# First attention of a two-block model: value products with the turned weights as stationary operand, and second-part copies on VectorE

## What is computed

```
for i in range(seq // 128):                       # 128 queries against (i + 1) * 128 keys
    z = q_i @ k[:kend].T / sqrt(64)
    mask = kpos < qpos
    log_beta = log_sigmoid(z)
    log_1m_beta = where(mask, log_beta - z, 0)
    suffix = cumsum(log_1m_beta, reverse=True) - log_1m_beta
    a = where(mask, exp(log_beta + suffix), 0)
    o_i = a @ v[:kend]
o = o * silu(z_gate);  x = x + gate * (o @ w_out)
```

## Time and profile before

| | us |
|---|---|
| median of 3 runs | 2759.29 (2758.49 to 2763.61) |
| the profiled execution, whole | 2765.38 |
| its span | 2763.6 |
| first attention in it | about 929.8 to 1210.5 |

### The profile page before, as it was taken

How to read it: one execution, slowest core, us unless ns; L and a number is a source line. 1 busy time by engine, 2 the same in 40 slices (tenths; PEclk the granted TensorE clock), 3 DMA queues, 4 the chain that set the end, 5 groups by cost and what they waited for, 6 DMA issues and landing times.

```text
span 2763.6 us, 34691 instructions
## 1 busy us (share of the span) xinstructions
PE 2596.2 (94%) x12363; PEld 2160.0 (78%) x12363; DVE 1548.8 (56%) x2099; ACT 1110.7 (40%) x1866; POOL 855.5 (31%) x626
## 2 busy tenths in 40 slices
PE   3899999999999999999899998789997999999998
PEld 2688888788778799987788877678875888887887
DVE  5666665641325466657764437775568777771112
ACT  3400001431411488856643437661265555551000
POOL 1233332012233466630132220233102323225664
PEclk7999999999999999999999999999999999999999
DMA  5244444344166544434253337414242333339933
GB/s 217 82 147 138 137 137 122 98 155 135 69 230 193 139 111 110 111 116 151 84 183 130 107 125 178 157 44 168 77 145 76 107 107 107 122 98 301 295 91 123
DMA packets 377272, 374.81 MB, mean 136 GB/s; under 512 B 36323, under 2 KB 284556, under 8 KB 376972
## 3 DMA queue, kind: packets, MB, share of 16 engines
q1 hardware_dynamic: 346844, 303.91, 37.0%
q10 hardware_dynamic: 30256, 68.69, 6.6%
HBM read 286.55 MB, written 85.98 MB: 135 GB/s over the span
## 4 chain that ended last, share of the span: by engine, by line
PE 75%; DVE 13%; ACT 5%; DMA 4%; issue 1%; POOL 1%; SPq 0%; ACTq 0%; DVEq 0%; POOLq 0%
PE PS L1743 27%; PE PS L1828 22%; PE PS L1897 8%; PE PS L801 5%; PE PS L779 2%; DMA mod_raw<-in_w_ada 2%; PE PS L1810 2%; PE PS L1787 1%; PE PS L765 1%; PE PS L764 1%; DVE opBf L2938 1%; DVE M L2599 1%; PE PS L1942 1%; DVE prob L1176 1%; ACT opBf L2085 1%
## 5 line engine op out<-in xcount | busy, mean ns | idle before, releaser
L1743 PE MATMUL PS<-opA,w_hi 128*128 128x512 f32 x2240 | 703.9, 394 | 12.2 <-POOL w_lo L1549 5.9
L1743 PEld LDWEIGHTS PS<-opA,w_hi 128*128 128x128 f32 x2240 | 425.2, 190 | 102.9 <-issue 7.3
L1743 PE MATMUL PS<-opA,w_lo 128*128 128x512 f32 x1120 | 439.8, 393 | 0.0
L1544 POOL CAST w_hi<-w_raw 128x1024 fp32r<-128x1024 f32 (+1 forms) x118 | 123.0, 1043 | 770.0 <-PE PS L1743 450.7
L1828 PE MATMUL PS<-opB,Xr 128*128 128x512 f32 x1120 | 308.7, 393 | 15.9 <-ACT M L2264 15.3
L1549 POOL TENSOR_TENSOR w_lo<-w_raw,w_hi 128x1024 fp32r<-128x1024 f32 (+1 forms) x120 | 290.8, 2424 | 83.6 <-ACT w_hi L2144 74.1
L1828 PE MATMUL PS<-opA,Xr 128*128 128x512 f32 x980 | 279.0, 395 | 6.5 <-DVE M L2955 3.4
L2599 DVE SCALAR_TENSOR_TENSOR M<-mod_raw,small,M 128x512 f32<-128x512 f32 x168 | 175.2, 1043 | 169.9 <-DMA mod_raw<-in_w_ada 85.3
L1828 PEld LDWEIGHTS PS<-opB,Xr 128*128 128x128 f32 x1120 | 212.1, 190 | 62.2 <-ACT M L2264 16.6
L1743 PEld LDWEIGHTS PS<-opA,w_lo 128*128 128x128 f32 x1120 | 212.6, 190 | 44.1 <-issue 0.2
L1828 PEld LDWEIGHTS PS<-opA,Xr 128*128 128x128 f32 x980 | 184.0, 190 | 51.1 <-ACT M L2264 8.0
(11 more groups left out here) (256 smaller groups left out, 4737.7 us busy)
## 6 DMA issues: line engine op xcount, KB each, us to landing
mod_raw<-in_w_ada SPq DMA_DIRECT2D x96, 256.0 KB, 2.9
z_dram<-opB ACTq DMA_DIRECT2D x44, 512.0 KB, 3.9
w_raw<-in_a_w_in SPq DMA_DIRECT2D x32, 512.0 KB, 4.9
hin<-q_dram SPq DMA_DIRECT2D x64, 256.0 KB, 5.8
w_raw<-in_w_down SPq DMA_DIRECT2D x32, 512.0 KB, 4.2
opA<-z_dram SPq DMA_DIRECT2D x60, 256.0 KB, 5.2
mod_raw<-in_b_mod_w SPq DMA_DIRECT2D x48, 256.0 KB, 2.8
X<-x_dram SPq DMA_DIRECT2D x24, 512.0 KB, 6.2
```

Source lines behind the costliest of these rows:

```text
L1544: pool.tensor_copy(hi, raw).then_inc(pool_done, 1)
L1743: ins = pe.matmul(ps, w[:, k0 + k, :], rhs(part, k0 + k), start=(k == 0 and n == 0), stop=(k == chunks - 1 and n == 2))
```

## The change

The value products exchange their operands: a_T of one item and one key block (128 keys x 128 queries) is now the stationary operand, and the 64 columns of that head's values move. The result has queries on partitions, 64 columns per item. A head's 8 items fill one bank (6 or 7 by the head's parity). DVE copies that bank into `rows_o` when the head is done, and when both heads of a pair are there PE transposes `rows_o` back in two halves of 4 blocks, through the same two banks, 4 and 5, that the transposes of a use; they are counted in one order with those (STICK_TURNS), and the bank of a half is free again when DVE's `finish` has read it. The copy of an item's second part goes from ACT to DVE. Values are loaded once per head pair, without clearing. The lags are TURN 4, VALUE 7, ROWS 8, BACK 9, OUT 10; half 1 of a pair is turned back 9 steps after the pair's last item, half 0 10 steps after.

```diff
-TURN_LAG, VALUE_LAG, OUT_LAG = 4, 7, 9
+TURN_LAG, VALUE_LAG, ROWS_LAG, BACK_LAG, OUT_LAG = 4, 7, 8, 9, 10
...
+def head_done(e):
+    return e // NT if 0 <= e < STICK_ITEMS and e % NT == NT - 1 else None
+def pair_done(t, lag):
+    for hf in (1, 0):
+        h = head_done(t - lag - (1 - hf))
+        if h is not None and h % 2:
+            return h // 2, hf
+    return None
+def stick_turns():
+    turns = []
+    for t in range(STICK_ITEMS + OUT_LAG + 2):
+        n = t - TURN_LAG
+        if 0 <= n < STICK_ITEMS:
+            turns += [("a", n, p) for p in range(stick_item(n)[1] // NQ + 1)]
+        if pair_done(t, BACK_LAG):
+            turns.append(("o",) + pair_done(t, BACK_LAG))
+    return turns
...
-        head_v = [at(f"head_v{i}", AT_B + (44 + 16 * i) * KIB, [T]) for i in range(2)]
+        pair_v = [at(f"pair_v{i}", AT_B + (44 + 16 * i) * KIB, [NT, 2, DH]) for i in range(2)]
         s_o = at("s_o", AT_M + 12 * KIB, [2, HALF])
+        rows_o = at("rows_o", AT_M + 12 * KIB, [NT, 2, DH])
...
+            def turn_free(c):
+                if c >= 2 and STICK_TURNS[c - 2][0] == "o":
+                    pe.wait_ge(dve_done, at("stick_o", *STICK_TURNS[c - 2][1:]))
+                elif c >= 2:
+                    pe.wait_ge(copied_by(STICK_TURNS[c - 2][2]), at("stick_hi", *STICK_TURNS[c - 2][1:]))
...
-                    if c >= 2:
-                        pe.wait_ge(act_done, at("stick_hi", c - 2))
+                    turn_free(c)
...
+            def values(n):
                 h, i = stick_item(n)
+                j, s = divmod(h, 2)
+                if n % (2 * NT) == 0:
+                    pe.wait_ge(value_in[j % 2], at("value_in", j))
+                for p in range(i // NQ + 1):
+                    pe.wait_ge(copied_by(p), at("stick_hi", n, p))
+                if h >= 2 and n % NT == 0:
+                    pe.wait_ge(dve_done, at("stick_rows", h - 2))
+                for kb in range(i + 1):
+                    ins = pe.matmul(PS[:, 6 + s, i * DH:(i + 1) * DH],
+                                    a_T[i // 2][kb // NQ][:, kb % NQ, n % 2 * P:n % 2 * P + P],
+                                    pair_v[j % 2][:, kb, s, :], start=(kb == 0), stop=(kb == i), skip_group_check=True)
...
+            def turn_back(j, hf):
+                c = STICK_PLACE["o", j, hf]
+                turn_free(c)
+                pe.wait_ge(dve_done, at("stick_rows", 2 * j + 1))
+                for b in range(NQ):
+                    ins = pe.transpose(PS[:, 4 + c % 2, b * P:(b + 1) * P],
+                                       rows_o[:, NQ * hf + b, :, :].rearrange("p s d -> p (s d)"), ident[:])
...
+                if 0 <= n - VALUE_LAG < STICK_ITEMS:
+                    values(n - VALUE_LAG)
                 if 0 <= n - TURN_LAG < STICK_ITEMS:
                     turn(n - TURN_LAG)
+                if pair_done(n, BACK_LAG):
+                    turn_back(*pair_done(n, BACK_LAG))
...
         def stick_dve(dve):
+            def second_copy(m):
+                c = STICK_PLACE["a", m, 1]
+                kbs = stick_kbs(m, 1)
+                dve.wait_ge(pe_done, at("stick_T", m, 1))
+                if m >= NT:
+                    dve.wait_ge(pe_done, at("stick_v", m - NT))
...
+                dve.tensor_copy(dst, src).then_inc(dve_done, 1)
...
+            def rows_out(h):
+                j, s = divmod(h, 2)
+                dve.wait_ge(pe_done, at("stick_v", NT * h + NT - 1))
+                if j:
+                    dve.wait_ge(pool_done, at("stick_out", j - 1, 0))
+                dve.wait_ge(dve_done, now(dve_done))
+                dve.tensor_copy(rows_o[:, :, s, :], PS[:, 6 + s, :].rearrange("p (b d) -> p b d", d=DH)).then_inc(dve_done, 1)
...
+            def finish(j, hf):
+                dve.wait_ge(pe_done, at("stick_back", j, hf))
...
+                dve.tensor_tensor(s_o[:, hf, :], PS[:, 4 + STICK_PLACE["o", j, hf] % 2, :], sz[:, j, hf * HALF:(hf + 1) * HALF],
                                   ALU.mult).then_inc(dve_done, 1)
...
+                if head_done(n - ROWS_LAG) is not None:
+                    rows_out(head_done(n - ROWS_LAG))
+                if pair_done(n, OUT_LAG):
+                    finish(*pair_done(n, OUT_LAG))
+                m = n - TURN_LAG
+                if 0 <= m < STICK_ITEMS and stick_item(m)[1] >= NQ:
+                    second_copy(m)
...
+                if h % 2 == 0:
+                    j = h // 2
+                    if j >= 2:
+                        sp.wait_ge(pe_done, at("stick_v", 2 * NT * (j - 1) - 1))
+                    sp.dma_start(pair_v[j % 2][:].rearrange("p b s d -> p (b s d)"), v_dram[j]).then_inc(value_in[j % 2], 16)
...
-                for e in range(2):
-                    other = head_v[e][:].rearrange("p (b s d) -> p b s d", b=NT, s=2)[:, :, 1 - e, :]
-                    pool.wait_ge(pool_done, now(pool_done))
-                    pool.memset(other, 0.0).then_inc(pool_done, 1)
```

More of the change, by code:

```diff
@@ L179 @@
 STICK_PIECES = stick_pieces()
-STICK_PLACE = {piece: c for c, piece in enumerate(STICK_PIECES)}
+def head_done(e):
[15 more added lines that the diff above has]
+    return turns
+STICK_TURNS = stick_turns()
+STICK_PLACE = {turn: c for c, turn in enumerate(STICK_TURNS)}
 SWA_STEPS = 2 * SWA_HEADS
@@ L733, in turn_v, with copied_by, stick_kbs @@
             step(pe_done, "v_T", u)
-        def stick_kbs(c):
-            n, p = STICK_PIECES[c]
+        def copied_by(p):
+            return dve_done if p else act_done
+        def stick_kbs(n, p):
             return range(NQ * p, min(NQ * p + NQ, stick_item(n)[1] + 1))
@@ L781, in turn @@
                     ins.then_inc(pe_done, 1)
-                    step(pe_done, "stick_T", c)
-            def values(n, part):
+                    step(pe_done, "stick_T", n, p)
+            def values(n):
                 h, i = stick_item(n)
[L787 to L807, removed]
@@ L811, in stick_pe @@
             pe.wait_ge(act_done, at("v_hi", U_QZ - 1))
-            for n in range(STICK_ITEMS + VALUE_LAG + 1):
+            for n in range(STICK_ITEMS + OUT_LAG + 2):
                 if n < STICK_ITEMS:
                     scores(n)
-                if n > VALUE_LAG:
-                    part = (n - VALUE_LAG) % 2 == 0
-                    values(n - VALUE_LAG - part, part)
+                if 0 <= n - VALUE_LAG < STICK_ITEMS:
+                    values(n - VALUE_LAG)
                 if 0 <= n - TURN_LAG < STICK_ITEMS:
                     turn(n - TURN_LAG)
+                if pair_done(n, BACK_LAG):
+                    turn_back(*pair_done(n, BACK_LAG))
         def piece_width(x, p):
@@ L984, in stick_act @@
         def stick_act(act):
-            for n in range(STICK_ITEMS + OUT_LAG + 1):
+            for n in range(STICK_ITEMS + OUT_LAG + 2):
                 if n < STICK_ITEMS:
@@ L992, in stick_act @@
                     if n >= BETAS:
[L993 removed]
+                        act.wait_ge(pe_done, at("stick_T", n - BETAS, stick_item(n - BETAS)[1] // NQ))
                     act.activation(beta[n % BETAS][:, 0:w], z, ACT.Sigmoid).then_inc(act_done, 1)
@@ L999, in stick_act @@
                 if 0 <= m < STICK_ITEMS:
[L1000 to L1009, removed]
+                    c = STICK_PLACE["a", m, 0]
+                    kbs = stick_kbs(m, 0)
+                    act.wait_ge(pe_done, at("stick_T", m, 0))
+                    if m >= NT:
+                        act.wait_ge(pe_done, at("stick_v", m - NT))
+                    dst = a_T[stick_item(m)[1] // 2][0][:, 0:len(kbs), m % 2 * P:m % 2 * P + P]
+                    src = PS[:, 4 + c % 2, 0:len(kbs) * P].rearrange("p (k q) -> p k q", q=P)
+                    act.activation(dst, src, ACT.Copy).then_inc(act_done, 1)
+                    step(act_done, "stick_hi", m, 0)
         def second_act(act):
@@ L1602, in stick_pool @@
                         step(pool_done, "stick_a", n)
-                    e = n - OUT_LAG
-                    if 0 <= e < STICK_ITEMS and e % NT in (5, 7) and e // NT % 2:
-                        finish(e // NT // 2, stick_item(e)[1] // NQ)
+                    if pair_done(n, OUT_LAG):
+                        finish(*pair_done(n, OUT_LAG))
             def second_pool():
```

36 lines of the change are left out of this document (14 added, 22 removed).

## The result

The changed kernel takes 2844.82 us (median, 2839.46 to 2846.46), the kernel before 2761.45 beside it: a ratio of 1.0297, 95% interval 1.0275 to 1.0318. It is 83 us slower, 18 us above the 2827 of the forecast and 2 us above the range's upper end. The profiled execution was the shortest of the four: 2839.46 us around a span of 2837.7.

What follows compares the result with a forecast made beforehand. The prediction took PE's own passes as the bound, with nothing covering a wait that stops PE. Its terms, 4.2 + 7.0 + 5.4 + 6.0 + 32.2 + 11.9 + 1.0 = 67.7 us, gave a median of 2827 us, range 2778 to 2843.

Steps and rivals of the forecast that it cites:

- Value products: First attention's value passes: 72 a head at 0.112 us, 8.06 us instead of 7.80, together +4.2 us.
- C: Rival on the value passes: a pass follows its columns, 0.054 us for 64; 2770 us, chance 0.04.
- Turning: Turning outputs back on PE: 8 transposes per pair, 64 at 0.109 us, +7.0 us.
- (a): Score banks: scores at position 4 wait for the scan at position 1, 0.67 us in 8 heads, +5.4 us.
- (b): Turning back half 1 waits for the bank ACT copies for item 4, 0.80 + 0.06 us, 7 times, +6.0 us.
- (c): Item 5's second transposes wait for DVE's finish of half 1 behind item 7's scan, 7 x 4.60 us, +32.2 us.
- (d): Clock: one half-clock stretch of 3.4 us behind each wait (c), 1.7 us lost, 7 times, +11.9 us; bounds 0 and 21.
- (e): End of the first attention: rows_out, drain and hand-over come before the next projection, +1.0 us.
- B: Rival on turning back: the turned-back half never makes PE wait; 2782 us, chance 0.12.
- C without the wait: Rival: value passes follow their columns and wait (c) is absent; 2730 us, chance 0.03.
- D: Rival: passes of half the columns leave PE at 1.2 GHz through the stage; 3045 us, chance 0.02.

Runs made afterwards that it cites:

- e3: The changed kernel with every value pass moving 128 columns instead of 64, the first attention not computed as in the reference; 2841.07 us, ratio 1.0279.
- e7: e6 with the copy of item 5's first part given to DVE, ahead of the 1024-column scan; 2798.55 us, ratio 1.0127.
- e1: The changed kernel with DVE's finish of a half one step earlier, ahead of the 1024-column scan; 2839.67 us, ratio 1.0272.
- e6: The changed kernel with second parts copied by ACT again and DVE's finish one step earlier; 2811.88 us, ratio 1.0178.
- e2: The changed kernel with 36 useless transposes filling each of the seven long PE gaps; 2819.19 us, ratio 1.0201.
- e5: The changed kernel with the copies of second parts given back from DVE to ACT; 2851.55 us, ratio 1.0322.
- e4: The kernel before with only the copies of second parts moved from ACT to DVE; 2773.57 us, ratio 1.0036.
- e8: The changed kernel with 18 useless transposes in each long PE gap, leaving seven gaps of 2.55 us; 2839.68 us, ratio 1.0278.
- e9: e6 with every value pass moving 128 columns, the first attention not computed as in the reference; 2808.76 us, ratio 1.0146.

## Why the prediction was wrong in size, point by point

**The sign and the mechanism held.** PE's passes and the waits between them set the time; nothing outside the stage moved.

**Value products, +4.2 forecast.** The pitch of 0.111 us for 64 columns held (0.97 us for eight), and rivals C fell with it and with e3. The sum did not: e7's plain head less its one wait is 17.02, as before, so the 0.26 us a head are not seen. They were the difference of 7.80 and 8.06, each a sum of many rounded prices, and 0.26 is 0.004 us for each of 72 passes: less than those prices bear.

**Turning, +7.0.** Eight transposes a pair; in after the next load starts 0.39 us behind the start of four of them (984.57 to 984.96), and 0.83 behind eight at the stage's end, against 0.44 and 0.87: held, a little cheaper.

**(a), +5.4.** Not in after, 0.68 a head in e7. The mechanism and size were right, the claim that no other wait stands in front was not.

**(b), +6.0.** 5.7 us in seven waits, 0.81 each against 0.86: held.

**(c), +32.2.** Seven gaps of 4.5 us, 33.3 us of the loads' waits, released by DVE's s_o L1174 right behind the scan: held. The heads were misnumbered by one: the pair's two heads are 2j and 2j+1, the lags put the step into the next pair's second head, so it is heads 3, 5, ... 15 and not 2, 4, ... 14. What e1 adds is that the gap was not only finish's doing: with finish out of the way the bank copies at the same place hold PE for 1.5 and 1.8 us. With finish and second copies both away from there (e6) the longest gap is 1.66 us and the full-clock head 20.42, so the order of DVE's queue is shown as the cause.

**(d), the clock, +11.9, bounds 0 and 21: this is the step that failed.** The prediction put one half-clock stretch of 3.4 us behind each wait (c), 1.7 us lost. In the profiled execution the seven stretches behind the gaps are 3.4, 10.2, 3.4, 10.2, 3.4, 6.8 and 10.2 us long. The six full heads among the seven are 154.3 us together where e2's are 139.7, so 14.6 us are lost, and 3.9 more in the last head (38.4 for 34.5): with head 0 it is 19.0 us between the two stages (357.0 and 338.0). Over all executions e2 gives 26. One stretch of 3.4 us behind a gap was the smallest case seen, not the usual one, and the upper bound took its length from a window of 6.0 us. The kernel before had longer ones that the prediction left out, one of them in head 0 of this very stage, behind a gap of 2.90 us, and one behind a gap of 4.08 us at the start of the second attention. Timeline and windows of before:

```profile
934.86 0.33 PE L764 MATMUL PS<-hin 128*128 128x128 f32 x1 [2.90 <-DVE M L1120]
...
935.70:942.50 6.80, 5.52 (x23) 5.08 (x23) 3.67 (x4) 3.72 (x10) 4.67 (x5) 0.50 0.01 3
...
1659.90:1669.60 9.70, 6.68 (x28) 6.11 (x28) 3.61 (x20) 3.89 (x11) 0.00 (x0) 0.50 1.10 310
```

**(e), +1.0.** The end of the stage, in the timeline of PEld in after, against the earlier trace rows:

```profile
1283.31 0.85 PEld L847 LDWEIGHTS PS<-ident,rows_o 128*128 128x128 f32 x8 [0.98 <-issue]
1284.14 0.19 PEld L1801 LDWEIGHTS PS<-opA,w_hi 128*128 128x128 f32 x1
```

A wait of 0.98, as forecast (the 0.83 of the eight transposes is in the turning).

**What was missing.** I wrote that DVE at 13.6 of 17.7 us is not the bound, which is true (12.65 of 18.46), and went on from there to price its copies at nothing. The waits for a bank at item 5's second part, at item 2 and at item 3, 0.31, 0.84 and 0.31 us of the loads' time, make a plain head 18.46 and not the forecast 17.95 (17.02 + 0.26 + 0.67) by adding 1.44 in place of 0.93. DVE's two are gone in e5 (which gains 0.37 a head, since the third grows), and the later of them is all of e4's cost; the third is ACT's: its first-part copy of item 5 stood at the same place before, and PE came there later. In the prediction I had looked at the score banks in just this way, for three steps that shrink from 5.74 to 4.93 us, and had not done so for the two transposition banks.

**The sum.** In the profiled execution, from heads' lengths: plain ones, 8 x 1.44 (heads 1, 2, 4, ... 14) and 1.0 for head 0, 12.5; six turned-pair heads at 23.29 against 17.02, 37.6; their clock 14.6; the last head with the tail, 38.4 against 27.1, 11.3. Together 76.0 of the measured 76.2.

Take the clock out and the forecast is 67.7 - 11.9 = 55.8 us. e2, whose gaps cost no clock, lies 2819.19 - 2763.37 = 55.8 us above the kernel before it. So the miss in size is the clock: with 26 in place of 11.9 the sum is 81.8, and 83.4 was measured. That the rest agrees to the tenth is luck: the value term and (a), 9.6 us together, are not in after, and the waits for the transposition banks that nobody had priced stand in their place.

The two spans differ by 74.1 us and the medians by 83.4, since after's profiled execution is 5.4 us below its own median and before's 3.9 above that of the runs beside after. Which part of that is clock this kernel's runs don't tell; e5's do: its four times go from 2840.09 to 2865.93 us and their granted clock from 0.966 to 0.958, the longest time with the lowest.

**The rivals.** B (no wait) is out by the seven gaps, C and C without the wait by e3, D (half clock for the stage) by a mean of 0.92.

## What to carry to other kernels

Where banks are used in turn, write down for every bank who frees it and what is queued ahead of that on its engine, for each place where the order of users or the length of the steps changes; an engine at 70% can hold PE for 4.5 us, or for 0.3 eight times. When a change puts idle time into PE, price the clock behind it with a wide bound above (here 26 us, where one short stretch a gap gave 12), and test it by filling the gap. In this kernel a float32 pass of 64 columns costs what one of 128 does, and one of 256 not quite twice that, so exchanging operands to move fewer columns than 128 bought nothing.

## What the runs showed of the hardware that was not expected

**Short gaps can cost the clock as well.** Gaps of 2.55 us were followed by 1.2 GHz in four of seven cases (e8), and in e6 gaps of at most 1.66 us in three heads of seven, for 10.2 us each. The Trainium skill, page "TensorE: Matmul & The Clock Gate", section "A second HAM failure mode: psum-queue depth-cycling", says of a bf16 kernel that frequent small idle times between groups of matmuls, with the PSUM banks cycled through, made the clock swing. e6 agrees in three heads, the first of them 25.27 us where 20.42 stands at full clock, and in four heads the same waits left the clock alone. In e9, with nearly the same waits, none fell. Why is open.

**The same program loses different amounts of clock.** Stretches of 3.4, 6.8 and 10.2 us stood behind equal gaps of 4.5 us in one execution of after, and e5's four times run from 2840 to 2866 us. What decides between them stays open, so the rows of before could have given the failed term a wider range, hardly its size.

**One, 64 and 128 moving columns have one pitch, 0.111 us**, in float32 (1 and 128 in the earlier trace rows, 64 in the eight loads of 0.97 us in after); 256 have 0.216.
